# Who multiplies the modulation's weights by silu(c): VectorE or GpSimd

## The reference, cut to what matters

```python
mod = jax.nn.silu(c) @ w_ada[l] + b_ada[l]                       # (1024) @ (1024 x 6144)
sh1, sc1, g1, sh2, sc2, g2 = jnp.split(mod[:, None, :], N_MOD, axis=-1)
u = rmsnorm(h, norm1_w[l]) * (1.0 + sc1) + sh1
...
h = h + g1 * mix
u = rmsnorm(h, norm2_w[l]) * (1.0 + sc2) + sh2
ff = (jax.nn.silu(u @ w_ffn_gate[l]) * (u @ w_ffn_up[l])) @ w_ffn_down[l]
h = h + g2 * ff
```

## Time and profile before

| what | value |
|---|---|
| time, median of 3 runs | 2111.33 us (2108.74 to 2111.37) |
| profiled execution, its own time | 2112.78 us |
| its span, first to last instruction | 2110.9 us |
| TensorE busy, share of the span | 92% |
| VectorE / ScalarE / GpSimd busy | 57% / 40% / 11% |
| mean granted TensorE clock | 0.97 of full speed |

### The profile page before, as it was taken

How to read it: one execution, slowest core, us unless ns; L and a number is a source line. 1 busy time by engine, 2 the same in 40 slices (tenths; PEclk the granted TensorE clock), 3 DMA queues, 4 the chain that set the end, 5 groups by cost and what they waited for, 6 DMA issues and landing times.

```text
span 2110.9 us, 25183 instructions
## 1 busy us (share of the span) xinstructions
PE 1947.0 (92%) x8972; PEld 1556.4 (74%) x8972; DVE 1209.8 (57%) x1650; ACT 838.5 (40%) x1098; POOL 229.6 (11%) x198
## 2 busy tenths in 40 slices
PE   5999999999999899999999998977488779999997
PEld 4877778888887677778888876766366558888885
DVE  4444345444689776554444788777756554444333
ACT  3665544443323444444444222444224334434221
POOL 2000020000112000010000122355312110000000
PEclk9999999999999999999999999988699889999998
DMA  3111123232455223122333454111021113322331
GB/s 127 61 56 44 49 80 101 98 99 99 142 192 179 80 95 97 58 101 89 99 99 97 162 180 154 60 40 40 20 80 60 40 60 100 99 99 94 94 94 48
DMA packets 56151, 193.57 MB, mean 92 GB/s; under 512 B 6944, under 2 KB 7456, under 8 KB 55968
## 3 DMA queue, kind: packets, MB, share of 16 engines
q1 hardware_dynamic: 48576, 165.05, 23.6%
q0 software_dynamic: 7520, 27.79, 4.0%
HBM read 186.52 MB, written 2.10 MB: 89 GB/s over the span
## 4 chain that ended last, share of the span: by engine, by line
PE 71%; DVE 14%; issue 9%; ACT 4%; POOL 1%; DMA 1%; SPq 0%; DVEq 0%; ACTq 0%; POOLq 0%
PE ps L341 20%; PE ps L343 20%; PE ps L342 20%; DVE wlo L326 2%; DVE tmps L762 2%; DVE wada L762 1%; DVE tmps L766 1%; PE ps L883 1%; PE ps L1725 1%; PE ps L901 1%; POOL qlev L1153 1%; PE ps L1730 1%; PE ps L1706 1%; PE ps L1742 1%; PE ps L922 1%
## 5 line engine op out<-in xcount | busy, mean ns | idle before, releaser
L341 PE MATMUL ps<-xh,whi 128*128 128x512 f32 x1536 | 609.3, 397 | 28.7 <-DVE xl L863 16.8
L343 PE MATMUL ps<-xh,wlo 128*128 128x512 f32 x1536 | 602.5, 392 | 0.0
L342 PE MATMUL ps<-xl,whi 128*128 128x512 f32 x1536 | 602.0, 392 | 0.0
L326 DVE TENSOR_TENSOR wlo<-raw,whi 128x1024 fp32r<-128x1024 f32 (+1 forms) x292 | 363.2, 1255 | 208.6 <-ACT whi L315 204.4
L315 ACT ACTIVATE whi<-raw 128x1024 fp32r<-128x1024 f32 (+1 forms) x304 | 310.5, 1036 | 223.6 <-PE ps L343 214.5
L341 PEld LDWEIGHTS ps<-xh,whi 128*128 128x128 f32 x1536 | 291.0, 189 | 102.0 <-issue 24.0
L343 PEld LDWEIGHTS ps<-xh,wlo 128*128 128x128 f32 x1536 | 290.7, 189 | 61.7
L342 PEld LDWEIGHTS ps<-xl,whi 128*128 128x128 f32 x1536 | 291.5, 190 | 59.5 <-issue 0.7
L341 PE MATMUL ps<-acth,whi 128*128 128x512 f32 x528 | 212.4, 402 | 0.2
L343 PE MATMUL ps<-acth,wlo 128*128 128x512 f32 x528 | 208.5, 395 | 0.0
L342 PE MATMUL ps<-actl,whi 128*128 128x512 f32 x528 | 208.3, 395 | 0.0
(11 more groups left out here) (256 smaller groups left out, 2392.4 us busy)
## 6 DMA issues: line engine op xcount, KB each, us to landing
raw<-in_gu SPq DMA_DIRECT2D x132, 512.0 KB, 3.3
raw<-in_down SPq DMA_DIRECT2D x48, 512.0 KB, 3.9
raw<-in_qkv SPq DMA_DIRECT2D x24, 512.0 KB, 4.2
wada<-in_ada POOLq DMA_DIRECT2D x24, 512.0 KB, 3.8
tmps<-in_ada POOLq DMA_DIRECT2D x24, 512.0 KB, 3.5
raw<-in_qkvb SPq DMA_DIRECT2D x24, 512.0 KB, 3.6
raw<-in_down SPq DMA_DIRECT2D x24, 384.0 KB, 3.1
raw<-in_recur SPq DMA_DIRECT2D x16, 512.0 KB, 3.4
```

The source lines that it names most:

```text
L326: eng.tensor_tensor(wlo[:, s, 0:n], raw[:, s, 0:n], whi[:, s, 0:n].bitcast(F32), ALU.subtract).then_inc(lo_done, 1)
L341: pe.matmul(ps[:, bank], whi[:, s, w], hi[:, k0 + k], start=start and k == 0, stop=False)
L342: pe.matmul(ps[:, bank], whi[:, s, w], lo[:, k0 + k], start=False, stop=False)
L343: mm = pe.matmul(ps[:, bank], wlo[:, s, w], hi[:, k0 + k], start=False, stop=stop and k == n - 1)
```

## The change

The multiplication with silu(c) moves from VectorE's queue into GpSimd's. `ada_product` on VectorE keeps only the sum over the 8 groups and waits on `ada_scaled`, which GpSimd now raises. In GpSimd's queue every transfer but the first two of a stage stands behind a product: product n, then the wait for the sum of tile n-1, then the transfer of tile n+1. Three products stand ahead of the addition of each output tile's square.

```diff
+        def ada_steps(pool, half, start, stop):
+
+            for n in range(24 * half + start, 24 * half + min(stop, 24)):
+                w = ada_w[n % 2].rearrange("p (k c) -> p k c", k=KT)
+                pool.wait_ge(ada_in[n % 2], 16 * (n // 2 + 1))
+                pool.tensor_tensor(w, w, csil.unsqueeze(2).to_broadcast((P, KT, P)), ALU.mult).then_inc(ada_scaled, 1)
+                if n % 24 >= 1 and n % 24 < 23:
+                    pool.wait_ge(ada_sum, n)
+                    pool.dma_start(ada_w[(n + 1) % 2], a["ada"][n + 1, :, :]).then_inc(ada_in[(n + 1) % 2], 16)
+
+        def ada_begin(pool, half):
+
+            for n in range(24 * half, 24 * half + 2):
+                wait(pool, ada_sum, n - 1)
+                pool.dma_start(ada_w[n % 2], a["ada"][n, :, :]).then_inc(ada_in[n % 2], 16)
+
         def pool_squares(pool, r, prior, ada=None):
 
-            def load_ada(start, stop):
-                for n in range(24 * ada + start, 24 * ada + min(stop, 24)):
-                    wait(pool, ada_sum, n - 1)
-                    pool.dma_start(ada_w[n % 2], a["ada"][n, :, :]).then_inc(ada_in[n % 2], 16)
-
             if ada is not None:
 
                 wait(pool, (f0, f1)[ada].lo, FT)
-                load_ada(0, 2)
+                ada_begin(pool, ada)
+                pool.wait_ge(set_a, 1)
...
             for m in range(KT):
                 if ada is not None:
 
-                    load_ada(3 * m + 2, 3 * m + 5)
+                    ada_steps(pool, ada, 3 * m, 3 * m + 3)
...
         def twin_squares_pool(pool):
...
             wait(pool, f1.lo, FT)
-            load_ada(0, 2)
+            ada_begin(pool, 1)
             for m in range(KT):
-                load_ada(3 * m + 2, 3 * m + 5)
+                ada_steps(pool, 1, 3 * m, 3 * m + 3)
...
         def ada_product(dve, half, t, j):
 
             n, par = t * 6 + (24 * half + j), j % 2
-            dve.wait_ge(ada_in[par], t * 48 + 16 * ((24 * half + j) // 2 + 1))
             w = ada_w[par]
-            dve.tensor_tensor(w.rearrange("p (k c) -> p k c", k=KT), w.rearrange("p (k c) -> p k c", k=KT),
-                              csil.unsqueeze(2).to_broadcast((P, KT, P)), ALU.mult).then_inc(ada_scaled, 1)
             dve.wait_ge(ada_scaled, n + 1)
             wait(dve, ada_done, n - 1)
             dve.reduce_sum(ada_part[par], w.rearrange("p (k c) -> p c k", k=KT), AX_X).then_inc(ada_sum, 1)
```

## The result

| | before | after |
|---|---|---|
| median of the runs | 2110.03 us (4 runs) | 2157.84 us (2152.75 to 2159.51, 4 runs) |
| span of the profiled execution | 2110.9 us | 2155.5 us |

The ratio is 1.0218, with a 95% interval of 1.0206 to 1.023: slower by 48 us. The forecast was 2174 us, slower, with a range of 2148 to 2217. Direction and range held; the loss was 63 us in the forecast and 48 in the measurement.

The account below looks back on a forecast made before the run. VectorE and TensorE were taken as nearly tied in the down stages; the change's serial GpSimd product-transfer loop would add 30.6 us in `down0` and 32.7 in `down1`, +63 in all, giving 2174 us, range 2148 to 2217.

Parts of the forecast that it names:

- The bound: Down stages: VectorE's 16.35 us and TensorE's 16.05 us per output tile almost tie, so relieving VectorE can't pay much.
- The 6.5 us: Down stages: all that can be won by taking 58 us of products from VectorE, 0.4 + 3.7 + 2.4.
- The loop: GpSimd's queue, down stages: product and transfer run serially with nothing overlapping, 2.37 + 3.8 = 6.17 us a turn.
- The term that was mis-sized: GpSimd's product in the down stages: 2.37 us each, taken from a two-input row of the same shape.
- cheaper, down to 1.45: Rival: GpSimd's product takes as little as 1.45 us, 44 us less, 2130 us, still slower than before; chance 0.06.
- the two cases: GpSimd's product at 2.37 us, as the forecast took it, or at 1.45 us, as the cheaper rival had it.
- the likeliest case: Down stages: the serial loop as worked out, 2174 us, own range 2158 to 2199; chance 0.70.
- The transfer: Down stages, GpSimd's queue: 3.8 us from issue to use, range 3.4 to 4.6, bare in 31 turns.
- The output tile's end: Product to addition's end: 5.6 us in `down0`, 1.8 beyond the landing, plus 0.5 contention; 7.25 us in `down1`.
- TensorE's clock: Rival, down stages: clock falls, free until three tenths of matmuls run at 1.2 GHz; half gives 2221 us; chance 0.05.
- A dearer product (3.68): Rival: GpSimd's product takes 3.68 us in the down stages, 63 us more, 2237 us; chance 0.12.
- The loop short enough for a gain: Rival: GpSimd's turn under 4.7 us in `down0`, 4.3 in `down1`, so VectorE's relief shows, at most 2105 us; chance 0.04.

Follow-up runs that it names:

- experiment 7: Kernel before with VectorE's product with silu(c) left out altogether; transfers, sums and small products stay: 2101.5 us, ratio 0.995.
- experiment 5: Changed kernel with a third buffer for the modulation's tiles, transfers issued behind a product but two tiles ahead: 2102.2 us, ratio 0.9965.
- Experiments 1: Changed kernel with the transfer of tile n+1 issued ahead of product n on GpSimd, once tile n-1 is summed: 2141.3 us, ratio 1.0149.
- 2: Changed kernel with GpSimd's additions of the squares one product later, behind product 3m+3 and the next issue: 2130.2 us, ratio 1.0093.
- 8: Kernel before, products on VectorE, with each transfer but a stage's first two issued only when product n-1 is over: 2139.5 us, ratio 1.0136.
- experiment 10: Changed kernel, GpSimd's product replaced: tile times itself or minus itself (2150 and 2155 us), or times the identity matrix (2177 us); one run each.
- experiment 3: Changed kernel with both edits: transfer issued ahead of the product, GpSimd's additions of squares one product later: 2124.8 us, ratio 1.0066.
- experiment 4: Changed kernel with transfer issued ahead of the product, additions one product later and cut from 512 to 8 columns: 2105.1 us, ratio 0.9975.

## Why the prediction was right, point by point

- **The bound.** That VectorE and TensorE are tied in these stages was right: 58 us of VectorE's work are worth 9 us (experiment 7). The 6.5 us were 2.6 short. That ceiling bounded what could be won; the sign hung on GpSimd's side, and experiment 5 turns it.
- **The loop.** Right in every step: the transfer is issued at a product's end, the next product waits for it, and the addition at an output tile's end comes after the landing. Experiments 1, 2, 5 and 8 each take hold of one link.
- **The term that was mis-sized** is GpSimd's product: 2.37 us taken, 1.89 measured (median of each of the two buffers' instructions). 48 x 0.48 = 23 us. The row that was taken has two full operands, and the product has one and 8 values (experiment 10). The prediction had this as a rival, "cheaper, down to 1.45", and gave it 0.06, with the argument that the repeated operand was no cheaper on VectorE. What holds on one engine didn't hold on the other: the truth lay between the two cases, a little over half of the way. The measured 2157.84 is just outside the likeliest case's own range (2158 to 2199). The stated range held because it reached 0.5 us into a cheaper product, and the product was 0.48 cheaper: near its edge, not in its middle.
- **The transfer.** 3.8 taken; the mean over the 31 turns in which it lay bare, 15 and 16 as forecast, was 3.92, with 3.46 to 4.65: +4 us. Right.
- **The output tile's end.** 5.6 us from product to the end of the addition, measured 5.75 (602.61 to 608.36); and the product behind it took 2.61 in place of 1.89, +0.72, where 0.5 was taken. Together +2.5 us over seven tiles. In `down1`, from the end of the product to the end of the second addition, 7.25 us were forecast and 7.24 measured (1246.59 to 1253.83), and the product behind took 1.90. With these three, 63 - 23 + 4 + 2.5 = 46.5 us; the stages show 45.2 and the medians 47.8.
- **TensorE's clock.** The granted clock did fall, to 0.91 and 0.93 in the windows above, from 1.00. In the first window that means 18% of the time (0.09 / 0.5) at the lower of the two levels, 1.2 GHz. It lies in two stretches, 600 to 604 (granted 0.55 and 0.59 in windows of 2 us) and 620 to 624 (0.67 and 0.50), and in the 2 us before the second one TensorE was busy for 0.55. An estimate: 3.6 us of a 20 us output tile at some 0.47 us a matmul (twice 0.233) are 8 of its 66 matmuls, where three tenths would have been needed. It cost nothing visible: in VectorE's timeline the addition to `h` at 604.53 starts right behind the sum, without a wait for TensorE.
- **The other rivals.** A dearer product (3.68) appeared only as the 2.6 us instances behind an addition. The loop short enough for a gain did not come, but experiment 5 shows what it needed: not a quicker product, a deeper ring.

## What to carry to other kernels

When work moves into the queue that also issues the transfers, write out that queue's order: an issue behind an instruction that waits for the previous landing turns two buffers into one. Work it out per turn, against the pace of the engine that really binds; here 48 products of 1.9 us cost nothing with three buffers, and 48 us with two and this order. A relief of an engine that is tied with another is worth only the difference, and leaving the work out altogether is a cheap run that tells it.

## What the runs showed of the hardware that was not expected

- A two-input instruction of GpSimd on 128 x 1024 f32 took 1.89 us when the second operand was 8 repeated values or the tile itself, 2.39 when it was a stream of its own (experiment 10). On VectorE the product with the 8 repeated values took 1.21 us, and so did `wlo` of the same shape in the kernel before:

```profile
623.28 1.21 DVE L326 TENSOR_TENSOR wlo<-raw,whi 128x1024 fp32r<-128x1024 f32 x1
```

- VectorE's two-input instructions can come almost to a stand while GpSimd's run: 2.8 us for 0.75 beside a product and an addition (experiment 3), 1.54 beside what was left of a product (experiment 4). The sum, with one input, kept its 1.98 us beside a product (experiment 5). It isn't always VectorE that gives way. In the changed kernel a `wlo` began beside the square's addition, and the product behind that addition was held up, 2.62 us in place of 1.89:

```profile
607.55 1.62 DVE L326 TENSOR_TENSOR wlo<-raw,whi 128x768 fp32r<-128x768 f32 x1 [0.35 <-ACT whi L315]
608.31 2.62 POOL L418 TENSOR_TENSOR tmps<-tmps,small 128x1024 f32<-128x1024 f32 x1
```

  In experiment 3 the addition behind the product kept its 1.29 us while `xl` stood. What decides between the two stays open.
